# A hybrid attention layer on one core: the first unit started on one k-tile, the memory's turns issued by GpSimd, the last tile in halves

## The reference, cut to what matters

```python
h = _rmsnorm(x, norm_g[l])
proj = h @ w_in[l]                                # 2048 x 18440
...                                               # A: dilated attention, 12 heads; B: forgetting, 8 heads
mh = _rmsnorm(mem, mem_norm_g[l])
km, vm = _split_cols(mh @ w_mem_kv[l], (M_WIDTH, M_WIDTH))
...                                               # M: cross-attention, 4 heads of 256
ua, ub, um = ...                                  # (branch output * silu(z)) @ w_proj
merged = g[:, :, 0] * ua + g[:, :, 1] * ub + g[:, :, 2] * um
x = x + (merged @ w_out[l]).astype(x.dtype)
```

## Time and profile before

| | us |
|---|---|
| median of 3 runs | 1171.43 |
| range of the runs | 1171.04 to 1172.53 |
| the profiled execution | 1171.77 |
| its span, first to last instruction | 1170.0 |
| PE busy in it | 1161.8 |
| DVE, ACT, POOL busy | 731.5, 546.1, 44.9 |

### The profile page before, as it was taken

How to read it: one execution, slowest core, us unless ns; L and a number is a source line. 1 busy time by engine, 2 the same in 40 slices (tenths; PEclk the granted TensorE clock), 3 DMA queues, 4 the chain that set the end, 5 groups by cost and what they waited for, 6 DMA issues and landing times.

```text
span 1170.0 us, 14507 instructions
## 1 busy us (share of the span) xinstructions
PE 1161.8 (99%) x5307; PEld 965.8 (83%) x5307; DVE 731.5 (63%) x906; ACT 546.1 (47%) x670; POOL 44.9 (4%) x37
## 2 busy tenths in 40 slices
PE   8999999999999999999999999999999999999998
PEld 7788888888888888888888888888888888888887
DVE  6776578576566577567567555655556456555653
ACT  6565445445444545545535544435434443543432
POOL 1110000000010000000000000000000000000000
PEclk9999999999999999999999999999999999999999
DMA  9998789658568678687677786477549546755860
GB/s 335 310 282 294 258 272 336 209 186 301 179 220 294 197 251 277 203 268 232 226 259 224 247 279 215 159 225 263 186 155 300 182 163 221 253 208 202 280 243 36
DMA packets 147613, 275.85 MB, mean 236 GB/s; under 512 B 9389, under 2 KB 32613, under 8 KB 147568
## 3 DMA queue, kind: packets, MB, share of 16 engines
q1 hardware_dynamic: 135488, 258.31, 66.0%
q10 hardware_dynamic: 11600, 16.87, 4.6%
q0 software_dynamic: 480, 0.07, 0.0%
HBM read 251.34 MB, written 26.24 MB: 237 GB/s over the span
## 4 chain that ended last, share of the span: by engine, by line
PE 96%; DMA 2%; SPq 1%; DVE 1%; issue 0%; ACT 0%; DVEq 0%
PE acc L1341 31%; PE acc L1342 31%; PE acc L1343 31%; DMA w_raw<-in_w_in_dram 1%; DMA turned_mem<-group 1%; PE side L1385 1%; PE side L1377 0%; PE side L1401 0%; PE side L1410 0%; PE side L1412 0%; PE side L1408 0%; PE side L1386 0%; SPq L308 0%; SPq L312 0%; DVE group L1079 0%
## 5 line engine op out<-in xcount | busy, mean ns | idle before, releaser
L871 DVE TENSOR_TENSOR w_lo<-w_raw,w_hi 128x1024 fp32r<-128x1024 f32 x407 | 495.8, 1222 | 372.1 <-ACT w_hi L551 371.4
L551 ACT ACTIVATE w_hi<-w_raw 128x1024 fp32r<-128x1024 f32 x407 | 429.6, 1060 | 540.8 <-PE acc L1343 524.0
L1341 PE MATMUL acc<-w_hi,hT_hi 128*128 128x512 f32 x1152 | 450.0, 391 | 0.4 <-DVE w_lo L871 0.4
L1343 PE MATMUL acc<-w_hi,hT_lo 128*128 128x512 f32 x1152 | 448.4, 389 | 0.0
L1342 PE MATMUL acc<-w_lo,hT_hi 128*128 128x512 f32 x1152 | 448.3, 389 | 0.0
L1341 PEld LDWEIGHTS acc<-w_hi,hT_hi 128*128 128x128 f32 x1152 | 216.3, 188 | 46.8 <-DVE w_lo L871 1.9
L1343 PEld LDWEIGHTS acc<-w_hi,hT_lo 128*128 128x128 f32 x1152 | 216.2, 188 | 45.3
L1342 PEld LDWEIGHTS acc<-w_lo,hT_hi 128*128 128x128 f32 x1152 | 216.3, 188 | 44.0
L1341 PE MATMUL acc<-w_hi,mT_hi 128*128 128x512 f32 x256 | 99.8, 390 | 0.0
L1342 PE MATMUL acc<-w_lo,mT_hi 128*128 128x512 f32 x256 | 99.6, 389 | 0.0
L1343 PE MATMUL acc<-w_hi,mT_lo 128*128 128x512 f32 x256 | 99.6, 389 | 0.0
(11 more groups left out here) (179 smaller groups left out, 573.0 us busy)
## 6 DMA issues: line engine op xcount, KB each, us to landing
w_raw<-in_w_in_dram SPq DMA_DIRECT2D x142, 1024.0 KB, 6.4
w_raw<-in_w_mem_kv_dram SPq DMA_DIRECT2D x16, 1024.0 KB, 5.5
w_raw<-in_w_out_dram SPq DMA_DIRECT2D x16, 1024.0 KB, 5.2
w_raw<-in_w_proj_a_dram SPq DMA_DIRECT2D x12, 1024.0 KB, 5.0
w_raw<-in_w_proj_m_dram SPq DMA_DIRECT2D x8, 1024.0 KB, 5.1
w_raw<-in_w_proj_b_dram SPq DMA_DIRECT2D x8, 1024.0 KB, 5.1
turned_oz<-group SPq DMA_DIRECT2D x44, 128.0 KB, 4.7
group<-turned_oz SPq DMA_DIRECT2D x11, 512.0 KB, 5.0
```

The lines of the kernel that those rows point to most:

```text
L551: act.activation(whi[:, s % RING], raw[:, slot, UK * (s % 2):UK * (s % 2) + UK], ACT.Copy)\
L871: dve.tensor_tensor(wlo[:, s % RING], raw[:, (s // 2) % RING, UK * (s % 2):UK * (s % 2) + UK], whi[:, s % RING].bitcast(F32), ALU.subtract ...
L1341: pe.matmul(banks[t][:], hi, whi[:, s % RING, j], start=first and j == 0, stop=False)
L1343: return pe.matmul(banks[t][:], lo, whi[:, s % RING, j], start=False, stop=last and j == UK - 1)
```

## The change

PE's list begins with two fillers, then block 0's k-tile 0 (which signals a semaphore of its own, `x0T`), `gx`'s transpose, k-tile 1, and seven fillers. Unit 0's first k-tile runs as six passes in the order high x high, low x high, high x low, each for both token halves and each pair behind its own wait (`first_tile`); block 1 is transposed behind it. Units 1 and 2 are split into k-tiles: ACT and DVE make their parts one k-tile at a time and PE waits for each (U_WHOLE). No load is changed. `mem_write` moves from SP's list to POOL's: turn 0 ahead of the first norm's power, turns 1 to 3 behind it and ahead of the second's. The keys are split at unit 31 instead of 29. In the scores the four full products go ahead of all split ones. In the last unit, token half 1 is done in two halves of 256 columns, the second in a bank of its own (`side[0]`); DVE adds the residual to both halves and then the last product to the second, ACT stores the first half and SP the second.

```diff
-U_QSPLIT, U_KSPLIT, U_VSPLIT, U_PSPLIT = 24, 29, 30, 15
+U_QSPLIT, U_KSPLIT, U_VSPLIT, U_PSPLIT = 24, 31, 30, 15
+U_WHOLE = 3
...
-                        if i in (7, 8, 10):
-                            mem_write((7, 8, 10).index(i))
...
-                            mem_write(3)
...
+            sp.wait_ge(chunk_taken, 2 * (4 * GROUPS + 6 * NCH + NCH - 1) + 4)
+            sp.dma_start(out_v[:, 1, D - CW // 2:], res[NCH - 1][:, 1, CW // 2:]).then_inc(last_out, 16)
+            sp.wait_ge(last_out, 16)
...
+            def mem_write(c):
+                pool.wait_ge(pre["mem_turned"], c + 1)
+                for i in range(4):
+                    rows = slice(32 * i, 32 * i + 32)
+                    pool.dma_start(mem_dram[c][:, i].rearrange("(j p) n -> p j n", j=4),
+                                   mem_squares[rows].rearrange("p (j n) -> p j n", j=4)).then_inc(pre["mem_out"], 16)
             for i in range(2 * M_GROUPS + 2):
+                for c in ((0,), (1, 2, 3))[i] if i < 2 else ():
+                    mem_write(c)
                 pool.wait_ge(means, i + 1)
...
+                if fixed(u0, 0) and s < U_WHOLE:
+                    for j in range(UK):
+                        act.activation(whi[:, s, j], raw[:, slot, UK * (s % 2) + j], ACT.Copy)\
+                           .then_inc(hi_done if j else pre["w_hi"], 1)
+                    return
...
-                act.wait_ge(pre["xT"], k // 2 + 1)
+                act.wait_ge(*((pre["xT"], k // 2 + 1) if k else (pre["x0T"], 1)))
...
+            result(NCH - 1, 0)
+            dve.wait_ge(tail_done, 2)
+            out_t = res[NCH - 1][:, 1]
+            for half in (slice(0, CW // 2), slice(CW // 2, CW)):
+                dve.scalar_tensor_tensor(out_t[:, half], acc[(NCH - 1) % 2][1][:, half], 0.5, out_t[:, half],
+                                         ALU.mult, ALU.add).then_inc(chunk_taken, 1)
+            dve.wait_ge(tail_done, 3)
+            dve.wait_ge(chunk_taken, 2 * (c + NCH - 1) + 3)
+            dve.scalar_tensor_tensor(out_t[:, half], side[0][:, half], 0.5, out_t[:, half],
+                                     ALU.mult, ALU.add).then_inc(chunk_taken, 1)
...
+            def first_tile():
+                toks = [slice(t * P, (t + 1) * P) for t in range(TT)]
+                pe.wait_ge(pre["x_hi"], 1)
+                pe.wait_ge(pre["w_hi"], 1)
+                for t in range(TT):
+                    pe.matmul(acc[0][t][:], hT[0][:, 0, toks[t]], whi[:, 0, 0], start=True, stop=False)
+                pe.wait_ge(pre["x_lo"], 1)
+                for t in range(TT):
+                    pe.matmul(acc[0][t][:], hT[1][:, 0, toks[t]], whi[:, 0, 0], start=False, stop=False)
+                pe.wait_ge(pre["w_lo"], 1)
+                for t in range(TT):
+                    pe.matmul(acc[0][t][:], hT[0][:, 0, toks[t]], wlo[:, 0, 0], start=False, stop=False)
...
+                    if early and s + j == 0:
+                        first_tile()
+                        tokens_T(1)
+                        continue
+                    if early:
+                        pe.wait_ge(*((lo_done, s + 1) if j else (pre["w_lo"], s + 1)))
...
+                    if step == 0:
+                        for h in range(4):
+                            pe.matmul(side[h][:, S:SEG], qT[:, 0, h], kT[:, 0, h], start=True, stop=True)
                     for h in (2 * step, 2 * step + 1):
                         for n, (x, y) in enumerate(((0, 0), (0, 1), (1, 0))):
-                            pe.matmul(side[h][:, 0:S], q2[x][:, h], k2[y][:, :, h], start=n == 0, stop=n == 2)
-                        o = pe.matmul(side[h][:, S:SEG], qT[:, 0, h], kT[:, 0, h], start=True, stop=True)
+                            o = pe.matmul(side[h][:, 0:S], q2[x][:, h], k2[y][:, :, h], start=n == 0, stop=n == 2)
...
+                        if k == 0:
+                            o.then_inc(pre["x0T"], 1)
+                            pe.wait_ge(g_in, 16)
+                            pe.transpose(acc[0][1][:, 0:KT], gx_rows, ident[0:KT, 0:KT]).then_inc(pre["gxT"], 1)
...
-            keep_clock(4)
-            pe.wait_ge(g_in, 16)
-            pe.transpose(acc[0][1][:, 0:KT], gx_rows, ident[0:KT, 0:KT]).then_inc(pre["gxT"], 1)
+            keep_clock(2)
             tokens_T(0)
-            keep_clock(9)
-            tokens_T(1)
-            keep_clock(2)
+            keep_clock(7)
...
+                for c0, bank in ((0, acc[n % 2][1]), (CW // 2, side[0])):
+                    half = slice(c0, c0 + CW // 2)
+                    for j in range(UK):
...
```

More of the change, by code:

```diff
@@ L266, in hybrid_block @@
     mixed, m_hi, m_lo = sem("mixed"), sem("m_hi"), sem("m_lo")
-    res_in, out_sem = sem("res_in"), sem("out_sem")
+    res_in, out_sem, last_out = sem("res_in"), sem("out_sem"), sem("last_out")
     pre = {n: sem("pre_" + n) for n in (
-        "half rel gains gxT gx gm sumx0 sumx1 sumx meanx rootx halfx xT x_hi x_lo wf_hi wf_lo dvec dvec_sb dvec_out w_hi w_lo "
+        "half rel gains gxT gx gm sumx0 sumx1 sumx meanx rootx halfx x0T xT x_hi x_lo wf_hi wf_lo dvec dvec_sb dvec_out w_hi w_lo "
         "summ meanm means_out means_in rootm mem_turned mem_out mem_back0 mem_back1 mem_back2 mem_back3 mT_hi mT_lo "
@@ L536, in hi @@
                 if fixed(u0, 0) and s == 0:
[L537 to L541, removed]
+                    token_hi(0)
+                    act.wait_ge(first_tile_in[0], 16)
+                    act.activation(whi[:, 0, 0], raw[:, 0, 0], ACT.Copy).then_inc(pre["w_hi"], 1)
+                    token_hi(1)
+                    act.wait_ge(first_tile_in[1], 16)
+                    act.activation(whi[:, 0, 1], raw[:, 0, 1], ACT.Copy).then_inc(hi_done, 1)
                     return
@@ L852, in _ @@
                     act.dma_start(out_v[:, :, n * CW:(n + 1) * CW], res[n]).then_inc(out_sem, 16)
-            for t in range(TT):
-                act.wait_ge(chunk_taken, 2 * (4 * GROUPS + 6 * NCH + NCH - 1) + t + 1)
-                act.dma_start(out_v[:, t, (NCH - 1) * CW:], res[NCH - 1][:, t]).then_inc(out_sem, 16)
+            taken = 2 * (4 * GROUPS + 6 * NCH + NCH - 1)
+            act.wait_ge(chunk_taken, taken + 1)
+            act.dma_start(out_v[:, 0, (NCH - 1) * CW:], res[NCH - 1][:, 0]).then_inc(out_sem, 16)
+            act.wait_ge(chunk_taken, taken + 2)
+            act.dma_start(out_v[:, 1, (NCH - 1) * CW:D - CW // 2], res[NCH - 1][:, 1, 0:CW // 2]).then_inc(out_sem, 16)
             act.wait_ge(out_sem, 16 * (NCH + 1))
@@ L1330, in _ @@
                             result(n, t)
-            for t in range(TT):
-                result(NCH - 1, t)
+            result(NCH - 1, 0)
[5 more added lines that the diff above has]
+            dve.wait_ge(tail_done, 3)
@@ L1335, in _, with passes @@
+            dve.wait_ge(chunk_taken, 2 * (c + NCH - 1) + 3)
+            dve.scalar_tensor_tensor(out_t[:, half], side[0][:, half], 0.5, out_t[:, half],
+                                     ALU.mult, ALU.add).then_inc(chunk_taken, 1)
         @block.tensor
         def _(pe):
-            def passes(s, x_pair, k, j, t, banks, first, last):
+            def passes(s, x_pair, k, j, t, banks, first, last, skip=False):
                 tok = slice(t * P, (t + 1) * P)
                 hi, lo = x_pair[0][:, k + j, tok], x_pair[1][:, k + j, tok]
-                pe.matmul(banks[t][:], hi, whi[:, s % RING, j], start=first and j == 0, stop=False)
-                pe.matmul(banks[t][:], hi, wlo[:, s % RING, j], start=False, stop=False)
-                return pe.matmul(banks[t][:], lo, whi[:, s % RING, j], start=False, stop=last and j == UK - 1)
+                pe.matmul(banks[t][:], hi, whi[:, s % RING, j], start=first and j == 0, stop=False,
+                          skip_group_check=skip)
+                pe.matmul(banks[t][:], hi, wlo[:, s % RING, j], start=False, stop=False, skip_group_check=skip)
+                return pe.matmul(banks[t][:], lo, whi[:, s % RING, j], start=False, stop=last and j == UK - 1,
+                                 skip_group_check=skip)
@@ L1345, in unit @@
             def unit(u0, s, x_pair, k, banks, first, last):
-                if not fixed(u0 + s if isinstance(u0, int) else u0, 0):
+                early = isinstance(u0, int) and u0 + s < U_WHOLE
+                if not early:
                     pe.wait_ge(lo_done, u0 + s + 1)
                 for j in range(UK):
-                    if isinstance(u0, int) and u0 + s == 0:
-                        pe.wait_ge(*((lo_done, 1) if j else (pre["w_lo"], 1)))
+                    if early and s + j == 0:
[4 more added lines that the diff above has]
+                        pe.wait_ge(*((lo_done, s + 1) if j else (pre["w_lo"], s + 1)))
@@ L1544, in _ @@
                 if s < NCH * CU - 1:
-                    unit(u0, s, mT, k, acc[n % 2], k == 0, k == KT - UK)
+                    unit(u0, s, mT, k, acc[n % 2], k == 0, k == KT - UK or s == NCH * CU - 2)
                     continue
```

(16 more changed lines are left out.)

19 lines of the change are left out of this document (13 added, 6 removed).

## The result

| | us |
|---|---|
| before, median of 4 runs beside it | 1171.81 |
| after, median of 4 runs | 1179.41 (1176.23 to 1180.63) |
| ratio after to before | 1.0059 (1.0047 to 1.0072) |
| the profiled execution of after, its span | 1176.23, 1174.1 |
| predicted | 1170.1 (1168.8 to 1172.6) |

The account below looks back on a forecast made before the run. TensorE (PE), busy 1161.8 of 1170.0 us, was taken as the bound, so only its waits could be won. Terms -0.26 - 0.70 - 0.10 - 0.25 = -1.31 from 1171.43 gave 1170.1 us (range 1168.8 to 1172.6).

Parts of the forecast that it names:

- First unit: Beginning: first matmul 1.06 us earlier, lead lost before unit 1, unit 2's wait gone: -0.26 us.
- Rival 3: First tile: TensorE's clock still at 1.2 GHz, unit 1 later, +1.2 in place of -0.26, 1171.5 us; chance 0.07.
- mem's first turn: GpSimd's fourth store issues at 34.3 and lands at 39.8, so the stall before unit 12 goes: -0.70 us.
- mem's second turn: Stores behind the first norm's power on GpSimd: fourth at 46.9, landing 52.4, with unit 15 not waiting.
- the 1.4 of cover: Before unit 15: its low part comes at 55.6 and is wanted at 57.05, so 1.4 us to spare.
- Rival 1: mem's turns: GpSimd's stores land late, each turn waits for the last; 1177 at 8.2 per landing; chance 0.07 beyond 7.1.
- mild form: mem's turns: GpSimd's landings take 5.9 to 7.1 us; at 7.0 the time is 1173.5; chance 0.11.
- The rule against it: mem's stores: VectorE's shared port blocks GpSimd's descriptor writes, unit 12's stall would stay, sum -0.6; not believed.
- The end: Last token half in two 256-column halves, last store 128 KB, landing 1169.3 instead of 1169.56: -0.25 us (-0.5 to +0.1).
- Scores and keys: Reordered score products have fewer changes of kind: -0.1 us (0 to -0.2); the keys' later split: nothing.

Follow-up runs that it names:

- run 1: The changed kernel with GpSimd's descriptor buffer at 1280 bytes per partition instead of 1024: 1173.31 us, ratio 1.0014.
- run 5: The changed kernel, buffer of 1024 bytes, each of mem's stores sent as two of 16 partitions with half the pieces: 1179.42 us in one execution.
- run 6: The changed kernel, buffer of 1024 bytes, with 34 unused transposes of the identity on TensorE ahead of unit 15: 1176.82 us, ratio 1.0047.
- run 9: The changed kernel, only mem's first turn on GpSimd, the rest on SP: 1171.08 and 1171.32 us; with twelve early zero products on TensorE as well: 1170.19.
- run 7: The changed kernel with the second turn's stores ahead of the first norm's power on GpSimd: 1171.00 us with 1280 bytes of buffer, 1172.03 with 1024.
- run 3: The kernel before with only mem's sixteen stores moved to GpSimd as in the change: 1178.39 us, ratio 1.0059.
- run 8: The kernel before with mem's sixteen stores on GpSimd and a buffer of 1280 bytes: 1173.47 us, ratio 1.0017.
- run 2: The changed kernel with mem's sixteen stores put back on SP, the rest of the change kept: 1170.51 us, ratio 0.9991.
- run 4: The changed kernel with GpSimd's descriptor buffer at 512 bytes per partition instead of 1024: 1181.91 us in one execution.

## Why the prediction was wrong, point by point

- **First unit: right at the early clock.** The first pass came at 7.30 (7.45 predicted), unit 1 at 11.96 with TensorE idle before it (12.2), the last transposes at 17.54 (17.75). The term reads -0.47 in this execution, of which 0.22 is TensorE's earlier start (3.98 against 4.20).
- **Rival 3, the lower clock in the first tile, was priced well and weighed badly.** In six of the ten profiled executions with the new beginning and no early products (runs 1, 5, 6, 9 twice and the 1024 of 7) the first tile ran at the lower level, and unit 1 came at 12.7 to 13.9 instead of 11.9 to 12.2: +1.1 in the mean, within the 1.0 to 1.4 given; the chance given was 0.07. The profiled execution of after was one of the four early ones. The late rise hits the old beginning too (run 3: transposes at 0.21 until 9.04, unit 1 at 12.79), but there it falls on fillers. Three profiles of the old beginning (near 7.6 in before, 9.3 in run 3, 7.8 in run 8) can't tell how often it is late.
- **mem's first turn: right.** Fourth store at 33.68, landing after 5.86 at 39.54 (34.3 and 39.8 predicted); VectorE's second turn at 39.63; unit 12 without a wait. Runs 7 and 9 keep this gain. The gain is read from the profiles; the medians do not show it (run 9). On SP the same store took 8.33 (run 2). The rule of the Trainium skill (DMA: Bandwidth & Descriptors, "Queues, rings and completion order") has the completion mark land after every earlier write of that DMA engine; that another queue would not escape SP's loads was the prediction's own conclusion from it. For this turn it is not borne out: in after the load that SP issued at 28.48 landed at 40.86, later than GpSimd's fourth store of 33.68 (39.54).
- **mem's second turn: the step that failed is "the fourth at 46.9, landing 52.4".** Its issue was priced at 0.58 like the three before it. It came at 53.36, 6.5 later, and landed at 57.80, 5.4 later than forecast; less the 1.4 of cover, that leaves 4.0 of the 4.1 that TensorE waited, so the cover was right. The prediction bounded how long a store takes to land, but not its issue. GpSimd's rows of before are of small loads that went one behind the other without a wait, and no row shows one that had to wait; the limit stood only in the line that creates the program.
- **The price of a stall was taken as its length.** A wait of 4.1 is followed by passes at half speed; with the stall filled they run at full speed (run 6), and the time is 1.4 us less by the ratios, 2.6 by the medians. No stall of before was long enough to show that.
- **Rival 1 named the right place and the wrong mechanism.** Its 8.2 per landing did not occur in these turns of after (5.86 and 4.45 at their fourth stores), so its 1177 is near the result by chance. Its mild form is real once the buffer is large enough: landings of 7.31 and 6.75, a wait at unit 18, 1173.3, where 7.0 was said to give 1173.5. That these agree so closely is in part chance, since 0.9 of run 1's profile is the clock of the first tile and 0.3 lies outside the span. The range, which ended at 1172.6, left out the prediction's own price for 7.0. Run 7 bears out that this comes from the place behind the power: sent there 4.5 earlier (41.19 against 45.73), the fourth store lands 4.85 after its issue, and unit 18 does not wait.
- **The rule against it** (SBUF — State Buffer, "SBUF: two separate sides" in the Trainium skill) did not decide: GpSimd's issues stayed at 0.54 to 0.61, and the longest wait fell where VectorE was busy 0.81 of 6.70 us and went with the buffer's size.
- **The end: right in sign, too small.** From unit 400 to the end of the span lie 24.99 to 25.03 us in the eleven profiles with the new end and 25.49 to 25.50 in the three without: -0.5 instead of -0.25, the edge of the bounds given. The last store of 128 KB landed in 2.0 (2.1 predicted), and VectorE's last 256 columns end at 1171.71, 0.88 after the last pass starts (1.12 before).
- **Scores and keys: nothing came of them.** No wait followed, and from unit 20 to unit 400, where all five groups lie, the profiles with the new order take 1072.20 to 1072.35 us and the three without it 1072.22 to 1072.37. The -0.10 is not there.

Added up by ratios: 1.0059 is 0.9991 (the change without the stores' move) and 0.0023 (the stores' move with a large buffer: later landings and 0.3 outside the span, and in run 1's profile also the late clock of the first tile, which is not the move's) and 0.0045 (the small buffer: the wait and the clock behind it). With the wait gone, the forecast's terms come together in the profile of run 7 with 1280 bytes: its span of 1168.4 is 1.6 below the 1170.0 of before, where 1.31 was forecast. Its median keeps 0.5 of that (1171.00 against 1171.48 beside it).

## What to carry to other kernels

Before moving DMAs to GpSimd, count their pieces in order against the buffer that the program reserves for them, those that have landed included: the eighth store had to wait although only three were under way. The one too many is issued only when the newest store under way has landed, and all that is queued behind it on GpSimd waits too. Enlarge the buffer (run 1), or place that wait where nobody needs the store soon (run 7). Bound the issue of a moved transfer as well as its landing, and add to a stall of 4 us of TensorE the passes at the lower clock behind it; those of 0.5 and 0.9 us in run 1 left the granted clock at 1.00. Where a new beginning puts real passes where fillers stood, it also takes over whatever clock these ran at, and early work without use can be cheaper than none (run 9, 1170.19 against 1171.32).

## What was not expected of the hardware

- GpSimd's stores wait in laps (7 at 1024 bytes, 3 at 512, 12 of half the pieces at 1024), and the wait is for the newest store under way, not for the oldest: the eighth, due at 46.6, went at 53.36, though the first of the three under way had landed at 50.06 and the second at 52.02. Stores that landed long before still take up their place in the lap.
- TensorE's step to 2.4 GHz comes at different times with equal beginnings: near 7.6 in before and near 9.3 in run 3; between 6.8 and 7.4 in the four early profiles of the new beginning and between 9.2 and 11.1 in the six late ones, with TensorE at work from about 4 us in each. With work from 1.2 us (run 9) it came at 6.3.
- The time outside the span is 2.1 us in after and runs 1, 3, 4, 6, 7 and 8, and 1.8 in before and runs 2, 5 and 9. What makes the 0.3 is open: run 5 has the most DMAs on GpSimd and 1.8.
